# Layer 0's scale row in four column quarters, with the weight chunks of the first block set between them

## The reference

```
cond = silu(c)                                  # c: 2048 numbers
shift, scale, gate = split(cond @ mod_w[i] + mod_b[i], 3)      # mod_w[i]: 2048 x 6144
h = rms_norm(x, norm_g[i]) * (1 + scale) + shift
# layer 0: out = pool_branch(h, pool_w_in, pool_w_grp, pool_scale, pool_w_out)
# layer 1: out = dsa_branch(h, ...)
x = x + gate * out
```

## Time and profile before

| what | us |
|---|---|
| median of 3 runs (2354.95 to 2356.41) | 2355.32 |
| the profiled execution, its own time | 2357.51 |
| its span in the trace | 2355.6 |
| TensorE matmul busy | 2308.8 (98%) |
| first scale row taken | 9.01 |
| first weight chunk started | 58.19 |

### The profile page before, as it was taken

One profiled execution on the slowest core, in us unless ns is written; L12 is line 12 of the kernel. 1 busy time (PEld: TensorE's weight loads), 2 busy tenths in 40 slices (PEclk: granted clock), 3 DMA queues, 4 the chain that ended last, 5 costly groups with the idle time before them and its releaser, 6 DMA issues.

```text
span 2355.6 us, 29822 instructions
## 1 busy us (share of the span) xinstructions
PE 2308.8 (98%) x10718; PEld 1870.5 (79%) x10718; DVE 1531.8 (65%) x1864; ACT 1134.6 (48%) x1371; POOL 298.3 (13%) x597
## 2 busy tenths in 40 slices
PE   6999999999999999999999999999999999999998
PEld 1877777888788878888888888888788888888886
DVE  2988888666797566775765444665665565565566
ACT  2444444454444456545455444454554444444444
POOL 0000000033300003200031000210221121121120
PEclk9999999999999999999999999999999999999999
DMA  9999997567698547756465766665676666666663
GB/s 393 398 373 378 378 397 253 186 194 215 216 391 268 166 150 235 232 179 187 140 203 167 240 192 193 212 199 169 213 216 204 201 212 196 207 213 195 209 209 112
DMA packets 263659, 547.14 MB, mean 232 GB/s; under 512 B 30188, under 2 KB 30452, under 8 KB 259576
## 3 DMA queue, kind: packets, MB, share of 16 engines
q1 hardware_dynamic: 241520, 510.40, 65.8%
q0 software_dynamic: 20368, 32.58, 4.2%
q10 hardware_dynamic: 1656, 2.66, 0.3%
HBM read 520.36 MB, written 6.30 MB: 224 GB/s over the span
## 4 chain that ended last, share of the span: by engine, by line
PE 79%; issue 10%; DVE 4%; DMA 3%; ACT 2%; POOL 1%; ACTq 0%; DVEq 0%; POOLq 0%
PE ps L2120 25%; PE ps L2122 25%; PE ps L2121 25%; POOL T L500 1%; DVE w_lo L1179 1%; DMA ifb<-in_f_bias 1%; PE ps L2204 1%; PE ps L2238 1%; DMA T<-T 1%; DMA T<-in_final_g 1%; ACT w_hi L569 0%; DMA wide<-gate_row 0%; PE ps L2308 0%; PE ps L2398 0%; PE ps L2421 0%
## 5 line engine op out<-in xcount | busy, mean ns | idle before, releaser
L1179 DVE TENSOR_TENSOR w_lo<-raw,w_hi 128x1024 fp32r<-128x1024 f32 x784 | 945.2, 1216 | 562.2 <-ACT w_hi L569 547.9
L569 ACT CAST w_hi<-raw 128x1024 fp32r<-128x1024 f32 x784 | 815.0, 1046 | 851.3 <-PE ps L2122 801.7
L2120 PE MATMUL ps<-w_hi,xa_hi 128*128 128x512 f32 x2176 | 854.3, 393 | 6.0 <-DVE w_lo L1179 4.9
L2122 PE MATMUL ps<-w_hi,xa_lo 128*128 128x512 f32 x2176 | 847.3, 389 | 0.0
L2121 PE MATMUL ps<-w_lo,xa_hi 128*128 128x512 f32 x2176 | 846.9, 389 | 0.0
L2120 PEld LDWEIGHTS ps<-w_hi,xa_hi 128*128 128x128 f32 x2176 | 408.5, 188 | 101.0 <-issue 9.7
L2122 PEld LDWEIGHTS ps<-w_hi,xa_lo 128*128 128x128 f32 x2176 | 408.5, 188 | 85.3
L2121 PEld LDWEIGHTS ps<-w_lo,xa_hi 128*128 128x128 f32 x2176 | 408.6, 188 | 83.0
L500 POOL DMA_DIRECT2D T<-T x576 | 283.0, 499 | 1170.1 <-DVE T L1279 1018.3
L2120 PE MATMUL ps<-w_hi,xb_hi 128*128 128x512 f32 x928 | 364.3, 393 | 2.2 <-DVE w_lo L1179 1.8
L2122 PE MATMUL ps<-w_hi,xb_lo 128*128 128x512 f32 x928 | 361.3, 389 | 0.0
(11 more groups left out here) (271 smaller groups left out, 998.2 us busy)
## 6 DMA issues: line engine op xcount, KB each, us to landing
raw<-in_w_in SPq DMA_DIRECT2D x176, 512.0 KB, 4.2
T<-in_mod_w SPq DMA_DIRECT2D x160, 512.0 KB, 7.4
raw<-in_attn_w_in SPq DMA_DIRECT2D x144, 512.0 KB, 4.7
raw<-in_w_up SPq DMA_DIRECT2D x128, 512.0 KB, 4.3
raw<-in_w_down SPq DMA_DIRECT2D x128, 512.0 KB, 4.7
raw<-in_pool_w_in SPq DMA_DIRECT2D x64, 512.0 KB, 7.9
T<-T POOLq DMA_DIRECT2D x576, 32.0 KB, 3.9
T<-in_mod_w SPq DMA_DIRECT2D x16, 1024.0 KB, 8.7
```

Of the source, the lines that this page charges most:

```text
L569: nc.scalar.copy(w_hi[:, o % SPL, :, 0:cols], raw[:, o % RAW, :, 0:cols]).then_inc(hi_ready, 1)
L1179: tt(w_lo[:, o % SPL, :, part], raw[:, o % RAW, :, part], w_hi[:, o % SPL, :, part].bitcast(F32), ALU.subtract).then_inc(lo_ready, 1)
L2120: mm(dst, x_hi, h, start=first and k == 0, stop=False)
L2122: ins = mm(dst, x_lo, h, start=False, stop=last and k == KPC - 1)
```

## The change

- The scale row is loaded and taken in four quarters of 512 output columns. A quarter is 8 pieces of 0.52 MB (two rows of 512 numbers per partition), in eight slots of T1 and T2; the last quarter uses six slots, so that its seventh and eighth piece wait for the first and second of the same quarter to be taken. On SyncE's queue two chunks of `pool_v` stand with each quarter, one after its seventh and one after its eighth piece.
- A piece is eight matmuls of 128 columns (`quarter_piece`), in banks 3 and 2 in turn. Each quarter's columns serve one `norm0` job.
- Of the first block, chunk 0 starts after quarter 0. Chunks 1, 3 and 5 are held: TensorE takes the eight pieces of quarter 1, 2 or 3 first, and turns the quarter's row into columns in the middle of the chunk. Chunks 2, 4 and 6 wait for the `norm0` job of that quarter.
- x comes on SyncE's queue in two transfers ahead of the pieces. The 13 vectors go to POOL's queue, ahead of its first memset. The positions and biases are issued by ScalarE after the root. The rotary steps stand on VectorE between the first and second quarter; the sine on ScalarE follows the second job.
- The first set of rides is four chunks later (into `group`). The eight TensorE rides of `group` are gone from there: all 32 lie in the gate and output phases. The shift row is summed after chunk 4 and turned after chunk 5 of `group`, and its four parts follow later on VectorE and ScalarE.

```diff
-    at = [v + c for c in range(4, 32) for _ in range(2 if c in (11, 17, 23, 28) else 1)]
+    at = [v + c for c in range(8, 36) for _ in range(2 if c in (11, 17, 23, 28) else 1)]
...
-    return at, [first["group"] + i for i in range(8)] + [gate + 1 + i * 60 // 24 for i in range(24)]
+    return at, [gate + 1 + i * 60 // 32 for i in range(32)]
...
+M_SLOT = [m % 8 if m < 24 else (m - 24) % 6 for m in range(M0)]
...
@@ sync
-            for k in range(KC):
-                if k >= 4:
-                    sp.wait_ge(mod_taken, k - 3)
-                sp.dma_start(mod_raw[:, k % 4, :], mws[0][:, 1, k, :]).then_inc(mod_landed[k % 4], 16)
+            for t, arrived in enumerate((x_landed, x_second)):
+                sp.dma_start(T0[:, t, :], x[0, t * P:(t + 1) * P, :]).then_inc(arrived, 16)
+            for m in range(M0):
+                if M_PREV[m] is not None:
+                    sp.wait_ge(mod_taken, M_PREV[m] + 1)
+                i, col, slot = m % 8, m // 8 * NBLK, M_SLOT[m]
+                sp.dma_start(mod_raw[slot].rearrange("p (k n) -> p k n", k=2), mws[0][:, 1, 2 * i:2 * i + 2, col:col + NBLK]
+                             ).then_inc(mod_landed[slot], 16)
+                if i >= 6:
+                    load(SOURCES["pool_v"], 0, m // 8 * 2 + i - 6, 0, first=True)
@@ scalar
-            phase("pool_v", pool_v, pool_job, first={2: norm0_start, 3: lambda: norm0(2), 5: lambda: norm0(3)})
+            phase("pool_v", pool_v, pool_job, first={4: lambda: norm0(2), 6: lambda: norm0(3)})
...
-                if o >= 6 and o < 10:
-                    shift0(o - 6)
+                if o >= 9:
+                    shift0(o - 9)
             mixed(3)
+            shift0(2)
+            shift0(3)
@@ vector
+            def quarter_scale(q):
+
+                bank, part = 3 - q % 2, slice(4 * q, 4 * q + 4)
+                dve.wait_ge(mod_taken, 8 * q + 8)
+                nc.vector.tensor_copy(q_raw[:, q * P:q * P + P], ps[:, bank, 0:P]).then_inc(q_rows, 1)
+                dve.wait_ge(q_sum, q + 1)
+                step(tt(scl[:, 0, part], ps[:, bank, S:S + 4], MODB[0][:, part], ALU.add))
+                step(tt(scl[:, 0, part], scl[:, 0, part], G0[:, part], ALU.mult))
+                dve.sem_inc(q_scl, 1)
+                norm0_low(q)
+
             lo(0, 0)
-            scale(0, 1, ps[:, 2, 0:KC], G0)
-            norm0_low(0)
+            quarter_scale(0)
             lo(0, 1)
-            norm0_low(1)
+            rotary_angles()
+            rotary_turns(cos, 0.25)
+            rotary_last()
             lo(0, 2)
+            quarter_scale(1)
...
-                          {3: lambda: norm0_low(2), 5: lambda: norm0_low(3)})
+                          {4: lambda: quarter_scale(2), 6: lambda: quarter_scale(3)})
...
-                4: shift_rows, 5: shift0_start, 6: lambda: shift0_next(0),
-                7: lambda: shift0_next(1), 8: lambda: shift0_next(2), 9: lambda: shift0_next(3)})
+                4: lambda: low_job(SPLITS["pool_v"] + 3, XB, 3, 4), 7: shift_rows, 8: shift0_start,
+                9: lambda: shift0_next(0), 10: lambda: shift0_next(1)})
+            shift0_next(2)
+            shift0_next(3)
@@ tensor
+            def quarter_piece(q, i):
+
+                m = 8 * q + i
+                pe.wait_ge(mod_landed[M_SLOT[m]], 16 * (M_LAP[m] + 1))
+                for k in range(2):
+                    col = csil[:, 2 * i + k:2 * i + k + 1].to_broadcast([P, 32])
+                    for r in range(4):
+                        at = k * NBLK + r * P
+                        ins = mm(ps[32 * r:32 * r + 32, 3 - q % 2, 0:P], col, mod_raw[M_SLOT[m]][:, at:at + P],
+                                 start=i == 0 and k == 0, stop=i == 7 and k == 1, skip_group_check=True)
+                ins.then_inc(mod_taken, 1)
...
+            for j in range(CPB):
+                if j == 0:
+                    pe.wait_ge(x_first, 1)
+                else:
+                    pe.wait_ge(x_ready, SPLITS["norm0"] + j // 2 + 1)
+                q = (j + 1) // 2
+                held = j in (1, 3, 5)
+                if held:
+                    if q >= 2:
+                        pe.wait_ge(q_scl, q - 1)
+                    for i in range(8):
+                        quarter_piece(q, i)
+                chunk(0, j, XA, KPC * j, 0, j == 0, j == CPB - 1, between=(lambda: quarter_columns(q)) if held else None)
+                if j in (1, 3):
+                    norm_job("norm0", 0, xn, 2 + j // 2)
...
-                if j == 1:
+                if j == 4:
                     pe.wait_ge(tp_evac, JOBS["pool_v"] + 3)
                     total_rows(0, 6)
-                if j == 2:
-                    mod_columns(2, 6, 0, False)
+                if j == 5:
+                    mod_columns(1, 6, 0, False)
```

More of the change, by code:

```diff
@@ L84, in _pe_slots @@
     late = sum(chunk < edge for chunk in PE_CHUNK)
-    slots = [4, 6, 5, 7] + [q % 4 for q in range(4, late)]
+    slots = [q % 4 for q in range(late)]
     slots += [(2, 3, 4, 5, 6, 7)[i % 6] for i in range(32 - late)]
@@ L99, in _pe_issue @@
     for q in range(32):
-        if q < 4:
-            g = group + 4 + q
-        elif PE_PREV[q] is None:
-            g = group + RAW + (4 if PE_SLOT[q] < 2 else 5)
+        if PE_PREV[q] is None:
+            g = group + RAW + (4 if PE_SLOT[q] < 2 else 7)
+            if PE_SLOT[q] >= 4:
+                g = PHASES["pool_out"][0] * CPB + RAW + 1
         else:
             g = PE_CHUNK[PE_PREV[q]] + RAW + 3
-            if PE_SLOT[q] >= 4 and PE_PREV[q] < 4:
-                g = PHASES["pool_out"][0] * CPB + RAW + 1
         at.append(max(g, at[-1]) if at else g)
@@ L112 @@
 PE_ISSUE = _pe_issue()
+M_SLOT = [m % 8 if m < 24 else (m - 24) % 6 for m in range(M0)]
+M_PREV = [max((p for p in range(m) if M_SLOT[p] == M_SLOT[m]), default=None) for m in range(M0)]
+M_LAP = [sum(M_SLOT[p] == M_SLOT[m] for p in range(m)) for m in range(M0)]
 RIDE_UNIT = (0, 2, 3)
@@ L265, in build @@
         amat = T[:, 2, 0:4 * NT * S].rearrange("p (g u t) -> p g u t", g=4, u=NT)
-        mod_raw = T[:, 1:3, :].rearrange("p a (s n) -> p (a s) n", n=D)
+        mod_raw = [T[:, 1 + s // 4, s % 4 * 1024:s % 4 * 1024 + 1024] for s in range(8)]
+        q_raw = probs_t[:].rearrange("p a n -> p (a n)")
         mod_acc = {0: T[:, 2, D:2 * D], 2: wide[:], 3: T[:, 2, 0:D], 5: wide[:]}
@@ L310, in build @@
         csil_ready, sin_in, rot_ready = sem("csil_ready"), sem("sin_in"), sem("rot_ready")
-        mod_landed = [sem(f"mod_landed{i}") for i in range(4)]
+        mod_landed = [sem(f"mod_landed{i}") for i in range(8)]
+        q_rows, q_sum, q_scl, x_second = sem("q_rows"), sem("q_sum"), sem("q_scl"), sem("x_second")
         ride_landed = [sem(f"ride_landed{i}") for i in range(4)]
@@ L2311, in pool @@
                 ins.then_inc(tp_ready, 1)
-            phase("pool_v", XA, pool, first=hooks, ready=SPLITS["norm0"], half=1)
+            for j in range(CPB):
[8 more added lines that the diff above has]
+                        pe.wait_ge(q_scl, q - 1)
+                    for i in range(8):
+                        quarter_piece(q, i)
+                chunk(0, j, XA, KPC * j, 0, j == 0, j == CPB - 1, between=(lambda: quarter_columns(q)) if held else None)
+                if j in (1, 3):
+                    norm_job("norm0", 0, xn, 2 + j // 2)
+            B0, A0, n = PHASES["pool_v"]
+            blk(B0 + 1, A0 + 1, XA, False, {3: lambda: pool(0)})
+            with pe.Fori(2, n) as b:
+                blk(b + B0, b + A0, XA, True, {3: lambda: pool(b - 1)})
             B0, A0, _ = PHASES["group"]
```

106 lines of the change are left out of this document (52 added, 54 removed).

## The result

The kernel after takes **2365.59 us**, the median of 5 runs (2363.99 to 2367.2), against 2355.32 in 5 runs of the kernel before (2354.95 to 2358.79). The ratio is **1.0039**, with a 95% interval of 1.0028 to 1.005: slower by 10 us in the medians, where the prediction had 2.3 us faster. That is above the whole stated range, 2346 to 2363, too. The profiled execution is the fastest of the five (2363.99, span 2362.2). Against the profiled one of before (2357.51, span 2355.6) it is 6.6 us of span longer, and it is these 6.6 us that the trace can explain.

The account below looks back on a forecast made before the run. TensorE (98% busy) was taken as the bound, with time to win only before its first chunk, which waited on DMA bytes. Start -5.0 and group stalls +2.7 gave -2.3 us, so 2353.0 us; range 2346 to 2363.

Parts of the forecast that it names:

- 5.0 us won: First block: chunk 8 was to start at 76.9 us instead of 81.94.
- the walk: Step-by-step timing of the quarters: last pieces taken at t1 = 35.3, t2 = 49.4, t3 = 65.8, chunk 8 at 76.9.
- Splitting rows in two costs no bandwidth here: Scale-row loads at the start: smaller pieces keep the DMA at 0.40 MB/us, as 0.5 MB chunk loads run at 399 GB/s.
- my lower bound of 0.57: Quarters: a piece of eight matmuls costs 0.57 us with one fixed part; the forecast took 0.72.
- Rival 2: First block and group: clock drops while TensorE waits; one drop 2356.4, one in each of three quarters 2363.2; chance 0.17.
- Chunks 8 and later ... have 4 us in hand: After the first block: chunks need 1.3 us of DMA apiece; 4 us spare since rides start four chunks later.
- 1.75 us lost: Group phase: with the later shift row, x is ready at 12.1 but TensorE is through chunk 7 at 10.4.
- 0.95 lost: Gate phase, chunk 3: remaining shifts hold w_lo to 22.85, while TensorE is there at 21.9.
- So nothing there, at worst 2: Behind group: 7 more pieces (9.2 us of DMA) fit, with 6.3 us more TensorE work and some 3 us of air.
- The first (the DMA's pace, 6.6 us won): Start: quarters run at DMA's pace if pieces cost 0.57 or less, chunk 8 at 72.6; 2346 to 2349; chance 0.30.
- The third (pieces bound by issue, 1.14): Quarters: pieces cost 1.14 us, chunk 8 at 84.0, 4.8 us lost with the group stalls, 2360.1; chance 0.10.
- The fourth: End of the pool layer: early win given back to DMA, change 0; counted in the forecast's chance of 0.43.

Follow-up runs that it names:

- best version with quarters: Run with eight slots (rides still four chunks later), but shift row and TensorE pieces as in the kernel before: 2355.73 us, ratio 0.9997.

## Why the prediction was wrong, point by point

**The account.** Every step between neighbouring kernels, by their ratios to the kernel before (0.001 is 2.36 us; each ratio is uncertain by about 0.001, so each step by 3 us or so):

| from, to | ratios | us |
|---|---|---|
| kernel before, quarters with eight slots, rides four chunks later | 1, 0.9997 | -0.7 |
| TensorE pieces out of `group` | 0.9997, 1.0009 | +2.8 |
| the shift row late | 1.0009, 1.0023 | +3.3 |
| six slots in the last quarter | 1.0023, 1.0039 | +3.8 |

From the other side, with the old start, the pieces cost 0.0013 (3.1 us) and late rides and shift row another 0.0021 (5.0 us); then the quarters give back 0.0011 (2.6 us), and the six slots cost 0.0016. Both ways the pieces and the shift row, with the rides, make 6 to 8 us of the 9 to 10.

**"5.0 us won" at chunk 8: the step that failed first.** It was 0.6. In the walk the last piece was to be taken at 65.8 and chunk 6 to start 5.65 later; they came 67.80, 2.0 late, and 7.97 later, 2.3 more. By its terms:

- *Rate.* "Splitting rows in two costs no bandwidth here" was wrong. The row I rested on, 399 GB/s, holds chunk loads of 2 KB runs and rides of 4 KB runs together. With 2 KB runs alone the rate is 386 to 387 in three kernels, two of quarters and the one with the old order of work; with 8 KB runs it was 419 at 28 to 48 us. In 16 to 24 us it is 335, and 330 in the old order too. Quarter 1's last piece was taken at 37.88 instead of 35.3. Eight slots brought the last piece to 65.35, where the DMA line of the prediction had landing at 60.6 and taking at 61.5. Of these 3.9 us the 387 makes 1.9 (23.0 MB at 0.387 end at 62.5); the rest goes with stretches in which less was moved, 320 GB/s at 16 to 24 us and 359 at 48 to 56 us in that run, the cause of which is open. The loss goes with the length of the runs and not with the size of the transfers: at 28 to 48 us those of 0.26 and of 0.52 MB, both with runs of 2 KB, went at 387 and 386 GB/s.
- *Slots.* The walk was right in kind: the seventh piece was issued at 61.18 (58.5 in the walk), the last two were taken at 65.09 and 67.80. The price is 2.45 us by the run with eight slots. In the walk it was 2.3, since with pieces at 0.72 the quarter would have been done at 49.4 + 14.1 = 63.5 without it.
- *Piece.* 3.26 us for seven pieces of quarter 2, so 0.47 at a clock of 1.00 and not 0.72: even under my lower bound of 0.57. It gained nothing, since TensorE then waited for the DMA (1.78 and 2.07 us ahead of the last two pieces).
- *Clock.* Rival 2 came true once in full: 0.50 at 68 to 72 us. It cost 1.8 us at chunk 6 (7.97 against 6.15 from the last piece to chunk 6), where my 3.4 for a drop came from a longer one: 0.83 over the 20 us from 380 on the earlier trace rows is 20 x 0.17 = 3.4 us of work, or 6.8 us at half. The drops that the runs showed up to pool job 0 cost 0.9 to 1.8 us each. A dip to 0.69 at 40 to 44 us cost 0.9 (chunk 2 at 44.90, and at 44.03 in the run with added matmuls, both with quarter 1's last piece at 37.88). The drops differ from execution to execution of the same instructions, and the one without any was only 0.2 us ahead of the run with eight slots by pool job 1: here they explain chunk 8, hardly the final time.
- *Right:* x, scalings (through by 19.4), the tiny loads (6.8 to 9.8 us, expected 6.5, and not the up to 26.5 of the earlier trace rows, which would have made the rotary steps late; at 18 to 20 us ScalarE's queue moved 293 packets beside 291 of SyncE's, one for one as in the earlier trace rows), the rotary steps at 30.1 to 36.5, chunk 0 within 2.1 us.

**"Chunks 8 and later ... have 4 us in hand".** They had not. VectorE waited 4.42 us for a ride to land, and TensorE 0.74 and 0.21 us behind it: 1.6 us with the restarts.

```profile
91.42 1.28 DVE L1480 SCALAR_TENSOR_TENSOR T<-T,csil 128x1024 f32<-128x1024 f32 x1 [4.42 <-DMA T<-in_mod_w]
```

The DMA had moved less in the first 70 us (349 GB/s against 393, which is 3.1 MB), and the debt stayed: by 103 us it was 365 against 395, again 3.1 MB. With eight slots the debt is smaller, and still it eats most: in the best version with quarters chunk 8 is 3.1 us ahead (pool job 0 at 89.70), 1.0 after the wait of 0.98 us at 101.24 (pool job 3 at 154.63), and 0.0 at the end mark (384.89 against 384.87).

**Group phase.** "1.75 us lost" and "0.95 lost": measured 1.66 and 0.85. This was right to 0.1 us. Together with their restarts they are most of what the late shift row costs: moving it early in the run with eight slots brought the end mark forward by 3.3 us (389.54 to 386.22), and 2.3 us of idle time in `group` and 0.4 at 347 to 375 us went with it. What the prediction left out of this phase is the DMA. Over 180 to 200 us, before and after (columns as in the earlier trace rows), and the waits of SyncE's queue from 178 to 195 us, before and after (line, waited for: us in total, times, longest):

```profile
180.00:200.00 20.00, 20.00 (x108) 14.23 (x107) 19.49 (x17) 7.22 (x8) 0.00 (x0) 1.00 0.99 360
180.00:200.00 20.00, 17.64 (x91) 12.85 (x92) 19.67 (x23) 8.92 (x9) 0.00 (x0) 1.00 0.62 205
```

```profile
SPq L385 <- DVE w_lo L1179: 8.2, 6, 3.1
SPq L389 <- DVE w_lo L1191: 16.0, 4, 6.3
```

A chunk load starts when VectorE's `w_lo` has read the slot. VectorE does the shift's chain instead, so the loads, and the rides queued behind them, stand still for up to 6.3 us, and 3.1 MB less are moved than before, some 8 us of the DMA at 400 GB/s.

**"So nothing there, at worst 2": the step that failed worst.** It put three microseconds of air at 270 to 300 us against 9.2 us of pieces. The air was real, and it is gone (399 GB/s there, 357 before). But that sum had no margin, and I took the DMA to start it without a debt. The waits at 350, 364 and 378 us (0.28, 0.80, 1.41) and their restarts are 3.4 us. Most of that is the pieces: without a hole at 180 to 200 us (304 and 382 GB/s), the old kernel with the pieces moved alone waits 1.55 us at 373, and the early shift row on eight slots still leaves 1.9 us. With the late shift row it is 2.3 to 3.0. Six pieces back in `group` end these waits, and all eight with the early row leave none, nor any in `group` but 0.68.

That TensorE waits for the DMA there, though the rows name `w_lo`, shows on VectorE. From 200 to 385 us it waits 6.0 us in all for rides to land in the kernel before and 6.5 in the best one with quarters, 10.4 with the pieces moved alone and 16.8 after. Nor does it take a hole in which an engine waits: with the pieces moved alone the DMA moved 282 GB/s at 140 to 175 us (370 before), TensorE waited only 0.18 us in `group`, and the 1.55 us came at 373. What the DMA has moved by 200 us puts the end marks in order, a hint and not a proof:

| kernel | mean GB/s, 0 to 200 us | end mark |
|---|---|---|
| best with quarters | 386 | 384.89 |
| before | 383 | 384.87 |
| eight slots, early shift row | 372 | 386.22 |
| before, pieces moved | 369 | 387.77 |
| eight slots | 366 | 389.54 |
| after | 360 | 392.75 |
| before, pieces, rides and shift row moved | 358 | 394.18 |

Of the other six kernels four fit this order within 0.2 us. Four pieces back in `group` (370, 390.11) ends later than its place, with the late load of 3.10 us, and the runs of 2 KB (378, 387.86) with a first chunk 3 us later.

**Rivals.** The first (the DMA's pace, 6.6 us won) had pieces under 0.57 right, but the DMA's pace was lower and the six slots cost 2.45; without them chunk 8 was 3.3 us ahead instead of 9.3. The third (pieces bound by issue, 1.14) is refuted by 0.47. The fourth, "given back to DMA at the end of the pool layer", named the mechanism, but I let it end at no change. The debt cost more than the start had won, because the same edit also cut what the DMA could do in between. My range had its slow end at three clock drops and none at this, which is why it missed. The sum of the trace, where the forecast had -5.0 + 2.7 + 0: -0.6 at chunk 8, +1.6 in `pool_v`, +3.1 for the two waits in `group`, +3.4 for the three at the layer's end, +0.4 in small waits, -1.3 in the switch, together +6.6.

## What to carry to other kernels

Here the DMA ran near its full rate through the whole layer (in the best version with quarters 386 GB/s up to 200 us and 387 from 200 to 370 us), and the earlier start of TensorE was worth only what the DMA could follow: 3.1 us at chunk 8 were 0.0 at the end of the layer. In such a kernel, sum the bytes up to the phase's end, and look for every stretch in which the edit leaves the load queue without free slots. Such a hole cost time here even where TensorE hardly waited in it (0.18 us in `group` with the pieces moved alone, and 1.55 at 373 us), and the bill came 150 to 230 us later. Before moving work "off" an engine into a later phase, count the transfers that it let through where it was: here eight small TensorE pieces gave the DMA a place for 4 MB.
